# The end of a one-step decoder kernel: the sample tile taken last, PSUM banks swapped, VectorE's order rearranged

## What is computed

```python
h2 = rmsnorm(x, norm2) * (1.0 + sc2) + sh2
ffn = moe(h2)                  # top 4 of 32 experts, clamped SwiGLU, gates by softmax
x = x + g2 * ffn
y_prompt = rmsnorm(yp, final_norm)
y_sample = rmsnorm(ys, final_norm)
```

## Time and profile before

| | us |
|---|---|
| median of 3 runs | 1273.93 |
| lowest, highest | 1272.82, 1274.53 |
| the profiled execution, its own time | 1273.49 |
| its span | 1271.7 |
| TensorE busy | 1250.2 (98%) |
| VectorE busy | 520.7 (41%) |
| ScalarE busy | 94.2 (7%) |

### The profile page before, as it was taken

One profiled execution on the slowest core, in us unless ns is written; L12 is line 12 of the kernel. 1 busy time (PEld: TensorE's weight loads), 2 busy tenths in 40 slices (PEclk: granted clock), 3 DMA queues, 4 the chain that ended last, 5 costly groups with the idle time before them and its releaser, 6 DMA issues.

```text
span 1271.7 us, 32191 instructions
## 1 busy us (share of the span) xinstructions
PE 1250.2 (98%) x14119; PEld 580.8 (46%) x14119; DVE 520.7 (41%) x823; ACT 94.2 (7%) x191; POOL 251.1 (20%) x336
## 2 busy tenths in 40 slices
PE   8999999899999999999999999999999999999996
PEld 7787754434333344444444444444444444444444
DVE  2033323583333333333334444444444443444447
ACT  5110011210000000000000000000000000000002
POOL 4502300112111111111221111111111111111111
PEclk9999999899999999999999999999999999999999
DMA  9555968299999999999999999999999999999996
GB/s 339 149 203 221 345 250 344 104 406 423 427 428 427 427 427 428 427 426 428 426 425 427 426 424 425 427 426 425 427 424 428 424 426 423 428 429 418 428 401 229
DMA packets 62963, 487.77 MB, mean 384 GB/s; under 512 B 10659, under 2 KB 19735, under 8 KB 37585
## 3 DMA queue, kind: packets, MB, share of 16 engines
q1 hardware_dynamic: 47826, 455.79, 86.0%
q0 software_dynamic: 11776, 21.02, 4.7%
q10 hardware_dynamic: 3327, 10.47, 2.1%
HBM read 468.48 MB, written 26.28 MB: 389 GB/s over the span
## 4 chain that ended last, share of the span: by engine, by line
PE 97%; DVE 1%; DMA 1%; ACT 1%; issue 0%; POOL 0%; DVEq 0%; POOLq 0%; ACTq 0%
PE acc L2198 51%; PE acc L2223 26%; PE acc L1015 9%; PE acc L1107 4%; PE acc L945 2%; PE acc L989 1%; PE acc L2176 1%; DMA raw<-expert_rows 1%; PE acc L966 0%; PE acc L1079 0%; ACT raw L1688 0%; PE acc L2324 0%; PE acc L2147 0%; DVE x_sb L1829 0%; PE acc L2309 0%
## 5 line engine op out<-in xcount | busy, mean ns | idle before, releaser
L2198 PE MATMUL acc<-raw_b,ht 128*32 128x512 f32 x2928 | 319.8, 592 | 0.0
L2198 PE MATMUL acc<-raw,ht 128*32 128x512 f32 x2928 | 319.8, 592 | 0.0
L1878 DVE TENSOR_TENSOR g_sb<-acc,bias_gu 128x768 f32<-128x768 f32 x32 | 30.6, 958 | 521.9 <-PE acc L2198 521.9
L1564 POOL DMA_INDIRECT rows<-h_rows,row_next x90 | 92.5, 1027 | 694.3 <-DVE row_next L1747 630.3
L2198 PEld LDWEIGHTS acc<-raw_b,ht 128*32 128x32 f32 x2928 | 95.4, 110 | 218.8 <-issue 218.8
L2198 PEld LDWEIGHTS acc<-raw,ht 128*32 128x32 f32 x2928 | 95.1, 110 | 205.7 <-issue 200.4
L2223 PE MATMUL acc<-raw_b,at 128*32 128x256 f32 x2976 | 166.3, 379 | 0.0
L2223 PE MATMUL acc<-raw,at 128*32 128x256 f32 x2976 | 166.3, 379 | 0.0
L2223 PEld LDWEIGHTS acc<-raw_b,at 128*32 128x32 f32 x2976 | 96.7, 110 | 77.1 <-issue 18.5
L2223 PEld LDWEIGHTS acc<-raw,at 128*32 128x32 f32 x2976 | 96.7, 110 | 63.9
L1015 PE MATMUL acc<-h_t,raw 128*128 128x256 f32 (+1 forms) x512 | 119.8, 395 | 0.4 <-DVE h_t L776 0.3
(11 more groups left out here) (303 smaller groups left out, 678.8 us busy)
## 6 DMA issues: line engine op xcount, KB each, us to landing
raw<-in_w_down SPq DMA_DIRECT2D x33, 2048.0 KB, 18.5
raw<-in_w_gate SPq DMA_DIRECT2D x31, 2048.0 KB, 13.0
raw<-in_w_up SPq DMA_DIRECT2D x31, 2048.0 KB, 17.4
raw_b<-in_w_gate SPq DMA_DIRECT2D x31, 2048.0 KB, 12.8
raw_b<-in_w_up SPq DMA_DIRECT2D x31, 2048.0 KB
raw_b<-in_w_down SPq DMA_DIRECT2D x31, 2048.0 KB, 18.5
raw<-in_w_ada SPq DMA_DIRECT2D x24, 1024.0 KB, 10.7
expert_rows<-zeros ACTq DMA_DIRECT2D x1, 8704.0 KB, 29.0
```

What stands on the lines that cost most here:

```text
L1564: pool.indirect_dma_start(rows[:, b, :], None, h2_quarter, bass.IndirectOffsetOnAxis(ap=idx[:, b:b + 1], axis=0), bounds_check=Q * NTOK - ...
L1878: dve.tensor_tensor(g_sb[:, :, :], gate_of(i, 0), plus(0), ALU.add).then_inc(g_read, 1)
L2198: mm = pe.matmul(gu_of(i)[b][q * TB:(q + 1) * TB, :].rearrange("p (m n) -> p m n", m=2), ht_of(i)[:, b, k, :], w[:, kk, :, q * CW:(q + 1) ...
```

## The change

The tiles are taken in the order 0, 1, 2, 3, PT by SP (loads and stores), TensorE and ScalarE. `LAST` stays tile 3, whose addition is still made in quarters. Tile 2 now uses banks 4 to 7 and tile 3 banks 0 to 3, so that each tile has the banks of the tile two ahead. ScalarE scales and stores the right half of tile 3 before it squares the samples. The matmul across the samples' quarters is TensorE's last. VectorE's list of calls is rearranged: `finish` is cut into `times_norm`, `inverse`, `whole_out` and `left_out`, and tile 2's reciprocal stands between the second and third quarter of tile 3, the samples' addition ahead of tile 3's reciprocal. The same follows in `again`, the repetition of the outputs that runs only if an expert has more tokens than its slots (left out below).

```diff
@@ -1434,16 +1434,21 @@
             y_at = [y_sb, u_sb]
-            tile_ps = [psum[:, 4 * i:4 * i + 4, 0:CW] for i in (1, 0, 0, 1)]
+            tile_ps = [psum[:, 4 * i:4 * i + 4, 0:CW] for i in (1, 0, 1, 0)]
             sample_ps = psum[:, 7, 0:CW]
             fin_ss_ps = psum[:, 4, 0:1]
             out_at = [ring_a[:, 2 * SLOT_F + t * D:2 * SLOT_F + (t + 1) * D] for t in range(TT)]
-            SEQUENCE = [0, 1, PT, 2, 3]
+            SEQUENCE = [0, 1, 2, 3, PT]
             AHEAD = 2
-            LAST = SEQUENCE[-1]
+            LAST = PT - 1
+            X2_AT = {0: 1, 1: 2, 2: 3, LAST: 3 + Q, PT: 4 + Q}
+
+            def sqrt_at(n, t):
+                return n * (TT + 1) + SEQUENCE.index(t) + (2 if t == PT else 1)
+
             STORES = 4 + Q + 1
             square_out = ring_a[:, 2 * SLOT_F + TT * D:2 * SLOT_F + (TT + 1) * D]
@@ -1489,7 +1494,7 @@
                 sp.wait_ge(y_stored, 16 * SB * (E - LATE))
-                for t in (0, 1, 2, PT, 3):
+                for t in SEQUENCE:
                     r = norm_rows(t)
                     if t == AHEAD:
                         sp.wait_ge(y_stored, 16 * SB * (E - 1))
@@ -1498,7 +1503,7 @@
                         sp.wait_ge(state_sent, 16 * (1 + DEC_T))
                     if t == 2:
                         sp.wait_ge(mm_done, pos(E - 1, 2 * MCH - 1) + 1)
-                    if t == PT:
+                    if t == LAST:
                         sp.wait_ge(mm_done, NCH * E - MCH)
                     rows_ = y_dram[TOPK * P * t:TOPK * (P * t + r), :]
                     if t < AHEAD:
@@ -1676,7 +1681,7 @@
                 def squares(n):
                     for i, t in enumerate(SEQUENCE):
                         r, k = norm_rows(t), n * TT + i
-                        act.wait_ge(x2_ready, i + (Q if t == LAST else 1))
+                        act.wait_ge(x2_ready, X2_AT[t])
                         if k:
                             act.wait_ge(fin_sq, k)
                         if t == PT:
@@ -1695,12 +1700,14 @@
                             act.wait_ge(fin_set, 3 + k)
                             act.activation(out_at[t][:, :], out_at[t][:, :], ACT.Identity,
                                            scale=fin_rstd[:, t:t + 1]).then_inc(out_ready, 1)
-                    act.wait_ge(fin_weighted, 2 * n + 2)
-                    act.wait_ge(fin_set, 2 + (n + 1) * TT)
-                    right = out_at[LAST][:, HALF:D]
-                    act.activation(right, right, ACT.Identity, scale=fin_rstd[:, LAST:LAST + 1]).then_inc(fin_sqrt, 1)
-                    act.wait_ge(fin_sqrt, (n + 1) * (TT + 1))
-                    act.dma_start(y_prompt[0, LAST * P:(LAST + 1) * P, HALF:D], right).then_inc(out_stored, 16)
+                        if t == LAST:
+                            act.wait_ge(fin_weighted, 2 * n + 2)
+                            act.wait_ge(fin_set, 3 + k)
+                            right = out_at[LAST][:, HALF:D]
+                            act.activation(right, right, ACT.Identity, scale=fin_rstd[:, LAST:LAST + 1])\
+                                .then_inc(fin_sqrt, 1)
+                            act.wait_ge(fin_sqrt, sqrt_at(n, LAST) + 1)
+                            act.dma_start(y_prompt[0, LAST * P:(LAST + 1) * P, HALF:D], right).then_inc(out_stored, 16)
                 def body(j):
                     act.wait_ge(ov_row_tp, j + 1)
@@ -1821,15 +1828,14 @@
                     dve.wait_ge(rows_summed, t + 1)
                     dve.tensor_tensor(x_sb[:, t, :], x_sb[:, t, :], rows_[:, 0, :], ALU.add).then_inc(x_added, 1)
+                def add_quarters(a, b):
+                    for q in range(a, b):
+                        dve.wait_ge(quarter_done, q + 1)
+                        x = by_quarter(x_sb[:, LAST, :])[:, q, :]
+                        dve.tensor_tensor(x, x, tile_ps[LAST][:, q, :], ALU.add).then_inc(x2_ready, 1)
+
                 def add_tile(t):
-                    if t == LAST:
-                        for q in range(Q):
-                            dve.wait_ge(quarter_done, q + 1)
-                            x = by_quarter(x_sb[:, t, :])[:, q, :]
-                            ins = dve.tensor_tensor(x, x, tile_ps[t][:, q, :], ALU.add)
-                            ins.then_inc(x2_ready, 1)
-                        return
-                    dve.wait_ge(tile_done, SEQUENCE.index(t) + 1)
+                    dve.wait_ge(tile_done, min(t, LAST) + 1)
                     if t == PT:
                         v = picked_at[t][:, 1, 0:QW]
                         dve.tensor_tensor(v, sample_ps, g2_sq[:, :], ALU.mult).then_inc(sum_step, 1)
@@ -2000,38 +2006,46 @@
                 y_add(E - 1, TOTAL)
                 add_rows(1)
-                def finish(n, t):
+                def times_norm(t):
+                    dve.wait_ge(x2_ready, X2_AT[t])
+                    dve.tensor_tensor(out_at[t][:, :], x_sb[:, t, :], fn_bc[:, :], ALU.mult).then_inc(fin_weighted, 1)
+
+                def inverse(n, t):
                     k = n * TT + SEQUENCE.index(t)
-                    if t >= LAST - 1 and t != PT:
-                        dve.wait_ge(x2_ready, TT - 1 + Q if t == LAST else SEQUENCE.index(t) + 1)
-                        dve.tensor_tensor(out_at[t][:, :], x_sb[:, t, :], fn_bc[:, :], ALU.mult).then_inc(fin_weighted, 1)
-                    dve.wait_ge(fin_sqrt, n * (TT + 1) + SEQUENCE.index(t) + 1)
+                    dve.wait_ge(fin_sqrt, sqrt_at(n, t))
                     dve.reciprocal(fin_rstd[:, t:t + 1], fin_ss[:, t:t + 1]).then_inc(fin_set, 1)
                     dve.wait_ge(fin_set, 3 + k)
                     if k == 0:
                         dve.wait_ge(fn_loaded, 16 * (1 + Q))
-                    if t == LAST - 1:
-                        return
-                    if t == LAST:
-                        dve.wait_ge(fin_weighted, 2 * n + 2)
-                        left = out_at[t][:, 0:HALF]
-                        dve.tensor_scalar(left, left, fin_rstd[:, t:t + 1], None, ALU.mult).then_inc(out_ready, 1)
-                        return
+
+                def whole_out(t):
                     x, fn, out_ = (x_q, fn_q[:, :], out_at[t][:, 0:QW]) if t == PT else \
                         (x_sb[:, t, :], fn_bc[:, :], out_at[t][:, :])
                     dve.scalar_tensor_tensor(out=out_, in0=x, scalar=fin_rstd[:, t:t + 1], in1=fn,
                                              op0=ALU.mult, op1=ALU.mult).then_inc(out_ready, 1)
+                def left_out(n):
+                    dve.wait_ge(fin_weighted, 2 * n + 2)
+                    left = out_at[LAST][:, 0:HALF]
+                    dve.tensor_scalar(left, left, fin_rstd[:, LAST:LAST + 1], None, ALU.mult).then_inc(out_ready, 1)
+
                 add_tile(0)
                 add_tile(1)
-                finish(0, 0)
+                inverse(0, 0)
+                whole_out(0)
+                inverse(0, 1)
+                whole_out(1)
+                add_tile(2)
+                times_norm(2)
+                add_quarters(0, Q // 2)
+                inverse(0, 2)
+                add_quarters(Q // 2, Q)
+                times_norm(LAST)
                 add_tile(PT)
-                finish(0, 1)
-                finish(0, PT)
-                add_tile(2)
-                finish(0, 2)
-                add_tile(3)
-                finish(0, 3)
+                inverse(0, LAST)
+                left_out(0)
+                inverse(0, PT)
+                whole_out(PT)
                 CHAIN = 15
...
@@ -2343,12 +2365,9 @@
                 late_expert(1, 1)
                 for t in SEQUENCE[AHEAD:]:
                     pe.wait_ge(x2_ready, SEQUENCE.index(t) - 1)
-                    if t == LAST:
-                        pe.wait_ge(fin_sqrt, SEQUENCE.index(PT) + 1)
                     late_expert(t, LATE - 1)
-                    if t == 2:
-                        across_quarters(0)
                     other_experts(t)
+                across_quarters(0)
                 blocks(pe, body, lambda: across_quarters(1))
```

More of the change, by code:

```diff
@@ L2100, in again @@
                 def again():
-                    for t in SEQUENCE:
-                        finish(1, t)
+                    for t in (0, 1):
+                        inverse(1, t)
+                        whole_out(t)
+                    times_norm(2)
+                    inverse(1, 2)
+                    times_norm(LAST)
+                    inverse(1, LAST)
+                    left_out(1)
+                    inverse(1, PT)
+                    whole_out(PT)
                 blocks(dve, body, again)
```

## The result

| | before | changed |
|---|---|---|
| median of 20 runs, us | 1273.62 | 1275.45 |
| lowest, highest | 1271.96, 1277.31 | 1273.56, 1277.99 |
| the profiled execution | 1273.49 | 1273.70 |
| its span | 1271.7 | 1271.9 |

The profiled execution of the changed kernel is one of its fastest, 1.75 us under its median, while that of before lies within 0.15 us of its median. This turned out to matter.

A forecast was written before the change was run, and what follows sets the result against it. Bound: arrival of tile 3's rows plus 9.4 us. Earlier rows give 1.7 us, ScalarE's tile 2 and VectorE's order take 0.3 and 0.7, the samples' tail ends 1.6 later: +0.9, median 1274.8 us, range 1273.0 to 1276.6.

The forecast's parts named there:

- tile 3's rows not earlier: Rival on SP's gathers: tile 3's rows still land at 1261.0; +2.6 us, 1276.5; chance 0.06.
- Tile 3's rows: Tile 3's gather, one place earlier on SP's queue, lands at 1259.3, between 1258.1 and 1259.8, instead of 1261.0.
- The strict queue: Rival on SP's queue: tile 3's load moves unmixed at 409 GB/s, landing 1258.1; -0.3 us, 1273.6; chance 0.20.
- Tile 2's banks: Tile 2 in banks 4 to 7: added at 1257.3, 2.7 us earlier, worth nothing by itself.
- The reciprocal inside the quarters: Tile 2's reciprocal on VectorE delays ScalarE's scaling, so tile 3's square starts at 1262.1, not 1261.8: 0.3 us given back.
- The samples' addition ahead of tile 3's reciprocal: VectorE's new order: tile 3's reciprocal starts at 1264.3 though its root is ready at 1263.6, 0.7 us late.
- From tile 3's rows to the samples' first store: Tail of the kernel: from rows landing at 1259.3 to the first of the samples' four stores at 1267.7.
- The samples' four stores: Kernel's end on SP: last issue 1269.0, last landing 1271.3 against 1270.4 before, +0.9 us.
- the quiet row: Four 32 KB stores at 241 us, taken for the samples' stores: starts spread over 1.3 us, landing in 2.3.
- the rival's 4.2 us to land: Rival on the samples' stores: 2.1 us of issuing, 4.2 to land, ending 1274.0; +3.6 us, 1277.5; chance 0.09.
- Tile 3's right half: Its store on ScalarE's queue: issued at 1265.3, landing 4.4 us later at 1269.7, 0.7 us earlier than before.
- TensorE does tile 3's late-expert part under the same cover: TensorE ahead of tile 3's rows: this work is hidden while the rows are awaited, with no cost counted.

The follow-up runs named there:

- d2: Changed kernel plus 12 matmuls nobody reads, on one strip of 32 rows, in the gap ahead of tile 3's fetched rows: 1.0075 against before, 1286.69 us.
- c4: Changed kernel with SP fetching the samples' rows ahead of tile 3's again, as before the change: 1.0036 against before, 1282.30 us.
- c1: The changed kernel again, nothing edited, for a second profile: 1.0019 against before, 1279.88 us.
- f3: The changed kernel once more, nothing edited, in the last group, for a third profile: 1.0019 against before, 1279.11 us.
- c2: Changed kernel with the samples' output in one store of 128 KB instead of four of 32 KB: 1.0027 against before, 1280.70 us.
- c3: Changed kernel with tile 3's reciprocal and left half ahead of the samples' addition on VectorE: 1.0007 against before, 1278.23 us.
- d1: Changed kernel with the samples' 12 late-expert matmuls in the gap ahead of tile 3's fetched rows: 1.0003 against before, 1277.79 us.
- d3: Changed kernel with the samples' late-expert matmuls in the gap and the end reordered on VectorE and ScalarE: 0.9990 against before, 1275.81 us.
- d4: d3 with two of the samples' four stores on ScalarE's queue: 0.9991 against before, 1276.13 us.
- f1: Changed kernel plus 12 matmuls nobody reads, over four strips of 32 rows, in the gap ahead of tile 3's rows: 1.0010 against before, 1278.66 us.
- f2: Changed kernel with tile 2's matmuls waiting until tile 1 is added too: 1.0007 against before, 1278.64 us.

## Why the prediction was right, and where it wasn't

The time (1274.8 forecast, 1275.45 measured) lies in the range, the side is the forecast one. The shift was +0.9 in the forecast, +1.8 in the medians. That the median is in the range is in part luck: the range's upper end came from a case (tile 3's rows not earlier) that didn't occur, and nothing in it was meant for what made up the second half of the difference. Step by step:

- **Tile 3's rows** were to land 14.3 us after tile 2's gather was issued (1259.3 less 1244.97); TensorE started on them after 14.06, and within 0.15 of that in every run with this order of gathers but d2, where the filler held it up. The strict queue, the rival of 1258.1, would be 13.1. In the first profile 388 GB/s were moved in the 6.0 us from tile 2's landing (1252.5) to tile 3's (1258.5), 2.33 MB where the load has 2.10: less beside it than the 0.42 MB before, but not nothing. With the old order of gathers (c4) they came at 15.58, so the place is worth 1.5 of the 2.0 us.
- **Tile 2's banks** were to be worth nothing, and so it is in the first profile: VectorE starts on its sum where tile 1's output ends. What they seem to cost is in the last point.
- **The reciprocal inside the quarters** was to cost 0.3 us, from ScalarE's scaling of tile 2: 0.36 at full clock (the square of tile 3 at 1261.34, the last quarter added at 1260.98), and nothing in c1's and f3's profiles, where the low clock makes the quarters later than the scaling.
- **The samples' addition ahead of tile 3's reciprocal** was to cost 0.7: 0.55 at full clock, 0.9 to 1.9 with the clock down (c1, c2, c4, f3); taking it away gave 1.5 us of time (c3).
- **From tile 3's rows to the samples' first store**: 8.4 forecast (1259.3 to 1267.7), 8.25 in the first profile.
- **The samples' four stores**: in the first profile their starts spread over 1.3 us and they took 1.8 to 2.8 us to land, as forecast from the quiet row. In the other profiles with four stores on SP the starts spread over 1.3 to 2.7 us and the landings took 1.6 to 3.3; the rival's 4.2 us to land didn't come. Tile 3's right half landed in 2.4 us and not in 4.4; it was issued 2.45 us ahead of the samples' first store and wasn't on the end.
- **The term that is missing** is in the sentence "TensorE does tile 3's late-expert part under the same cover": I put TensorE's work ahead of the rows at nothing, and didn't ask what the empty stretch behind it does. It became 2.3 to 2.6 us long (it was 0.8). Six profiles have it (c4's is 3.9), and in five of them the clock fell to half within that wait or within tile 3's matmuls: 1.5 to 1.8 us in the distance where VectorE's order is the change's (c1, c2, c4, f3, against 8.25). The exception is the first profile of the changed kernel. In the five profiles with the gap filled or divided (d1, d3, d4, f1, f2) it never fell before the samples' matmuls on fetched rows were done. How often it falls in executions without a profile isn't known, so that it makes up the missing 1.1 us of the result is inferred and not seen; by my estimate a fall in some two thirds of them would make the mean 0.7 + 1.1 = 1.8, the difference of the medians.

So the forecast is right for an execution at full clock (f1, which has the same order and keeps the clock, is at 1.0010, 1.3 us; f2 at 1.0007, 0.9 us), and about half of the measured difference comes, as far as these runs show, from a mechanism that it didn't have. What exactly makes the clock fall they leave open: in the first profile the same gap did nothing.

## What to carry to other kernels

When work is brought forward into a wait, ask what the engine does in the longer wait that follows. The empty stretch ahead of matmuls on the critical path cost more here (1.5 to 1.8 us, where the clock fell) than the order of single operations did at full clock (0.36 and 0.55); matmuls that have to be done anyway fill it best. And when the profiled execution lies away from the median of its kernel, take a second profile before explaining the median with the first, and compare the stretch that was changed, from a mark ahead of it: what lies before the tail differed here by 5.4 us among three profiles of the changed kernel.

## What the runs showed that I hadn't expected

- Float32 matmuls of 32 rows by 256 columns that go round the four strips of 32 rows take 1.58 us for 12; on a single strip (and with three banks instead of four), 8.15 us, part of it at half clock. In the 2.5 us at full clock (1260.5 to 1263.0) 11 of the 24 records ran, 0.22 us each, against 0.066.
- On a single strip the clock fell while TensorE was counted busy (d2, above); what it is that the chip goes by, these runs leave open.
- One store of 128 KB to a pattern of four column blocks is no faster than four of 32 KB, though it needs 0.70 us of issue instead of 2.85 (c2 and c1).
